# Four buffers for the projections' weights, constants issued by GpSimd, and a new order at three places of a fused block kernel

## The chip, the cores and the metric

The kernel runs on one core of one Trainium2 chip, in a single launch. The metric is the time of an execution on the device in microseconds (us); lower is better. The core has five engines that matter here: TensorE (PE in the profile, PEld for its weight loads), VectorE (DVE), ScalarE (ACT), GpSimd (POOL) and SyncE (SP, which only issues transfers). Each engine works through its own list of instructions in order and waits on semaphores. Transfers are issued from the queues of SP, ScalarE and GpSimd.

## The reference

Two transformer blocks, one after the other, on 1024 tokens of width 1024, all in float32; the second has 256 context tokens in front (1280 rows in all, in 10 tiles of 128). The change touches these pieces:

```python
# three projections, each with a residual and a norm (proj1, proj2, proj3)
x = layer_norm_affine(ALPHA * x + gate1 * (y @ w_o[l]), ln1_g[l], ln1_b[l])
y_l = concatenate([ret_o, rw_o], axis=-1) @ w_out          # even layer
# preparation of the recurrence
def token_shift_mix(u, mu):
    prev = jnp.pad(u[:, :-1], ((0, 0), (1, 0), (0, 0)))
    nxt = jnp.pad(u[:, 1:], ((0, 0), (0, 1), (0, 0)))
    return u + mu * (0.5 * (prev + nxt) - u)
w_log = -jax.nn.softplus(-(w0[d] + jnp.tanh(wd[:, :, d]) @ w2[d])) - 0.5   # low rank 64
a = jax.nn.sigmoid(a0[d] + ad[:, :, d] @ a2[d])                            # low rank 64
# recurrence in two directions, then a norm per head, a bonus and a gate
gn = ((rw_y - mean) * lax.rsqrt(var + RWKV_GN_EPS)).reshape(bl, l, RWKV_W) * rw_ln_w + rw_ln_b
rw_o = (gn + bonus.reshape(bl, l, RWKV_W)) * jax.nn.silu(u[..., E_WZ:E_SHIFT])
```

## The kernel before

`program` runs some twenty stages one after the other, with a barrier of all engines between two. In a stage each engine runs the same hand-written order of steps (`in_order`), takes the steps that concern it, and waits on counting semaphores. The change touches three stage functions.

**project_stage** is called three times (proj1 with `w_o`, proj2 with `even_w_out`, proj3 with `odd_w_out`). It multiplies 8 or 10 tiles of 128 rows by a 1024 x 1024 weight, in split precision: a weight chunk of 128 x 1024 (8 chunks, 512 KB each) is loaded into `raw` (2 buffers, loads at L639), copied to `w_hi` by ScalarE (L723) and subtracted into `w_lo` by VectorE (L772); chunk k may be loaded when `w_lo` of chunk k-2 is done. Each tile of x is transposed on TensorE ("turn", L679), split into `y_hi` (ScalarE, L731) and `y_lo` (VectorE, L811), and multiplied ("mult", three products per chunk, L690 to L692) in two halves of 512 columns; for tile 0, half 0, TensorE waits for `w_lo` chunk by chunk. ScalarE copies the product to `r` (L745), GpSimd multiplies it by the gate (L651), VectorE adds the residual `res` (loads at L628) and norms it ("norm", L822 on), and TensorE transposes it back ("back", L699). The order is turn 0, turn 1, mult 0, turn 2, norm 0, mult 1, back 0, and so on. With `gates` (proj3 alone) ScalarE first takes the silu of a second input z (L719), for tiles 0 and 1 before everything else, for tile t+2 within mult t, and VectorE multiplies it onto x (L768). The constants (gate rows, each sent to all 128 partitions, and columns of scale, shift and weight as 1024 single elements each) are issued from ScalarE's queue ahead of its other work (L706 to L714); VectorE's `fold` (L778) uses them after the last `w_lo`. proj1 has five of them, proj2 eight, proj3 two.

**rwkv_prep_stage** mixes each of 10 tiles with its neighbour rows (loads of `near` at L2245 and L2248; "shift" L2434 to L2441, "mix" L2444), makes four low-rank products ("lora", L2365; of the sequence 0,0 0,1 1,0 in step lora and 1,1 in step lora_end, through a ring of three banks), takes their sigmoid ("lora_out"), and fills the waits with other work in `slot`s: a small network with two sines ("sine", L2330 and L2427), eight scalings of filter products by a decay table ("filter" L2338 on TensorE, "scale" L2505 on VectorE, tables loaded at L2259 into two buffers), and 16 spectra ("spec", 16 matmuls each, L2350; "spec_out" L2521). Two boundaries of the sequence fall into tiles 1 and 2: there one neighbour row comes from elsewhere, and the other 127 rows are one load.

```python
for t in range(NTA):
    more = t + 1 < NTA
    yield "slot", SLOTS * t
    ...
    yield "lora_end", t
    yield "lora_out", t
    if more:
        yield "shift", t + 1
    yield "slot", SLOTS * t + 1
```

**rwkv_stage** runs 20 units (10 tiles, two directions) through a software pipeline, `PERIOD`: pairs of a step and how many units ahead it runs. T1_out (L3064) and X2 (L2857) lie on the chain of a unit, as does the trip of the inverse through memory (inv_out L2722, inv_in L2731, then X0, L2840). Behind it the two directions of a tile are added, normed per head, and gated in the y_ steps, for tile number k in the order `DONE`, in the iteration `GATED[k]`: y_load, y_load_z (SP, L2740, L2747), y_center (L3071 to L3077), y_square, y_var, y_root (ScalarE, with the silu of z before it), y_scale, y_end (L3090 to L3096, stored by GpSimd, L2784).

## Time and profile before

| | |
|---|---|
| median of 3 runs | 5418.17 us (5416.61 to 5421.66) |
| the profiled execution's own time | 5423.96 us |
| its span | 5422.3 us |
| mean granted TensorE clock | 0.891 of full speed |
| TensorE (PE) busy | 4482.0 us (83%), 26314 instructions |
| VectorE (DVE) busy | 2563.2 us (47%) |
| ScalarE (ACT) busy | 1400.6 us (26%) |
| GpSimd (POOL) busy | 643.7 us (12%) |
| proj1, proj2, proj3: first load issued at | 1048.67, 4012.53, 5277.12 us |
| preparation, recurrence: first load issued at | 2901.94, 3276.61 us |

The profile is of one execution. Times in it are microseconds from its start. A line such as L690 is a line of the kernel, printed above. "idle before <- releaser" names what ended the idle time of an engine; SPq and ACTq are the queues from which SP and ScalarE issue transfers, and the time of such a row is that of the issue alone.

### The profile page before, as it was taken

How to read it: one execution, taken by the hardware profiler on the slowest of the kernel's cores; microseconds unless marked ns; L12 is line 12 of the kernel's file. 1: busy time of each engine (PE TensorE's matmuls, PEld its weight loads, DVE VectorE, ACT ScalarE, POOL GpSimd, SP SyncE). 2: the span in 40 equal slices, each digit the busy share in tenths (PEclk: the TensorE clock that was granted, in tenths of full speed). 3: DMA queues.
4: the chain of work that ended last, by engine and by line, in shares of the span. 5: the costliest groups of instructions: out<-in, count | busy, mean ns of one | idle time of the engine just before them, and what ended most of it. 6: DMA issues, size and time to landing. Idle time of an engine off the chain costs nothing. (4 is left out here: it accounts for less than half of the span.)

```text
span 5422.3 us, 70452 instructions
## 1 busy us (share of the span) xinstructions
PE 4482.0 (83%) x26314; PEld 3681.0 (68%) x26314; DVE 2563.2 (47%) x4721; ACT 1400.6 (26%) x2867; POOL 643.7 (12%) x704
## 2 busy tenths in 40 slices
PE   5999998677998992499955686999848999886877
PEld 3998886566887882499943234888846999334546
DVE  3567774653433004311145675777534255343655
ACT  3232234432221001211122232344324111002333
POOL 1111111210000001000012012111111134110001
PEclk8999997788999996699976688999769999888998
DMA  4444433412112012222122554343332344333014
GB/s 151 164 146 146 133 110 140 169 66 58 48 46 65 30 37 105 88 79 78 56 94 105 190 216 126 99 113 105 82 107 102 124 165 173 138 129 103 8 29 142
DMA packets 430205, 578.47 MB, mean 107 GB/s; under 512 B 186461, under 2 KB 325590, under 8 KB 425256
## 3 DMA queue, kind: packets, MB, share of 16 engines
q1 hardware_dynamic: 367037, 403.73, 23.6%
q0 software_dynamic: 45280, 163.46, 7.9%
q10 hardware_dynamic: 17616, 7.66, 0.6%
q8 instruction: 171, 2.80, 0.2%
q14 instruction: 101, 0.82, 0.0%
HBM read 412.89 MB, written 161.86 MB: 106 GB/s over the span
## 5 line engine op out<-in xcount | busy, mean ns | idle before, releaser
L336 PE MATMUL g_in_g_acc<-g_in_g_whi,g_in_hi 128*128 128x444 f32 (+4 forms) x960 | 355.8, 371 | 16.4 <-DVE g_in_g_wlo L326 9.9
L337 PE MATMUL g_in_g_acc<-g_in_g_wlo,g_in_hi 128*128 128x444 f32 (+4 forms) x960 | 345.1, 359 | 0.0
L338 PE MATMUL g_in_g_acc<-g_in_g_whi,g_in_lo 128*128 128x444 f32 (+4 forms) x960 | 344.7, 359 | 0.0
L212 PE MATMUL g_even_acc<-g_even_w_hi,h_hi 128*128 128x384 f32 (+1 forms) x960 | 317.2, 330 | 30.2 <-DVE g_even_w_lo L254 30.2
L212 PE MATMUL g_down_acc<-g_down_w_buf,fT 128*128 128x256 f32 x1408 | 306.2, 381 | 16.4 <-DMA g_down_w_buf<-in_w_down 16.4
L214 PE MATMUL g_even_acc<-g_even_w_lo,h_hi 128*128 128x384 f32 (+1 forms) x960 | 317.1, 330 | 0.0
L215 PE MATMUL g_even_acc<-g_even_w_hi,h_lo 128*128 128x384 f32 (+1 forms) x960 | 317.1, 330 | 0.0
L212 PEld LDWEIGHTS g_down_acc<-g_down_w_buf,fT 128*128 128x128 f32 x1408 | 268.9, 191 | 53.7 <-DMA g_down_w_buf<-in_w_down 16.8
L336 PE MATMUL g_odd_g_acc<-g_odd_g_whi,h_hi 128*128 128x344 f32 (+3 forms) x816 | 264.9, 325 | 32.2 <-DVE g_odd_g_o L356 16.5
L337 PE MATMUL g_odd_g_acc<-g_odd_g_wlo,h_hi 128*128 128x344 f32 (+3 forms) x816 | 263.0, 322 | 0.0
L338 PE MATMUL g_odd_g_acc<-g_odd_g_whi,h_lo 128*128 128x344 f32 (+3 forms) x816 | 262.2, 321 | 0.0
L1784 DVE SCALAR_TENSOR_TENSOR up_cv<-up_acc,up_taps,up_cv 128x1023 f32<-128x1023 f32 x88 | 112.8, 1282 | 280.6 <-ACT up_cv L1760 273.3
L1739 PE MATMUL up_acc<-h_hi,up_w_hi 128*128 128x512 f32 x704 | 219.1, 393 | 8.7 <-DVE up_w_lo L1777 8.7
L230 DVE COPY g_even_o_buf<-g_even_acc 128x384 f32<-128x384 f32 (+1 forms) x60 | 32.1, 535 | 399.2 <-PE g_even_acc L215 399.2
L336 PEld LDWEIGHTS g_in_g_acc<-g_in_g_whi,g_in_hi 128*128 128x128 f32 x960 | 182.4, 190 | 56.0 <-issue 27.7
L1739 PE MATMUL up_acc<-h_lo,up_w_hi 128*128 128x512 f32 x704 | 220.2, 394 | 0.0
L1739 PE MATMUL up_acc<-h_hi,up_w_lo 128*128 128x512 f32 x704 | 218.0, 391 | 0.0
L1588 DVE SCALAR_TENSOR_TENSOR g_in_m_acc<-g_in_m_w,g_in_c_act,g_in_m_acc 128x256 f32<-128x256 f32 x448 | 201.8, 481 | 22.3 <-issue 1.9
L690 PE MATMUL proj_acc<-proj_w_hi,proj_y_hi 128*128 128x512 f32 x416 | 176.2, 424 | 32.7 <-DVE proj_w_lo L772 32.7
L212 PEld LDWEIGHTS g_even_acc<-g_even_w_hi,h_hi 128*128 128x128 f32 x960 | 181.5, 189 | 30.6 <-DVE g_even_w_lo L254 30.6
L338 PEld LDWEIGHTS g_in_g_acc<-g_in_g_whi,g_in_lo 128*128 128x128 f32 x960 | 182.4, 190 | 7.5
L337 PEld LDWEIGHTS g_in_g_acc<-g_in_g_wlo,g_in_hi 128*128 128x128 f32 x960 | 182.6, 190 | 6.5
(542 smaller groups left out, 9914.7 us busy)
## 6 DMA issues: line engine op xcount, KB each, us to landing
g_in_m_w<-in_ada_w SPq DMA_DIRECT2D x24, 1024.0 KB, 5.3
up_w_buf<-in_w_up SPq DMA_DIRECT2D x44, 512.0 KB
U2p<-g_even_o_buf POOLq DMA_DIRECT2D x11, 1920.0 KB, 7.8
g_odd_x<-U3p SPq DMA_DIRECT2D x24, 768.0 KB
g_even_w_buf<-in_even_w_in SPq DMA_DIRECT2D x11, 1536.0 KB
g_in_m_w<-in_w_ada SPq DMA_DIRECT2D x16, 1024.0 KB, 6.2
prep_near<-U2p SPq DMA_DIRECT2D x18, 896.0 KB
PD<-prep_od POOLq DMA_DIRECT2D x10, 1536.0 KB, 8.7
```

The costliest lines, as they stand in the source:

```text
L212: mm = pe.matmul(o, hi[:, k, tt], w_hi[:, par, k, :wd], start=k == 0, stop=not split and k == kc - 1)
L214: pe.matmul(o, hi[:, k, tt], w_lo[:, par, k, :wd], start=False, stop=False)
L215: mm = pe.matmul(o, lo[:, k, tt], w_hi[:, par, k, :wd], start=False, stop=k == kc - 1)
L230: op = eng.tensor_copy(o_buf[:, par, t, :wd], acc[bank][:, :wd])
L336: pe.matmul(bank[:, :wd], hi[:, k, tt], w_hi[:, st % 2, k, :wd], start=k == 0, stop=False)
L337: pe.matmul(bank[:, :wd], hi[:, k, tt], w_lo[:, st % 2, k, :wd], start=False, stop=False)
L338: op = pe.matmul(bank[:, :wd], lo[:, k, tt], w_hi[:, st % 2, k, :wd], start=False, stop=k == KC - 1)
L690: pe.matmul(acc[t % 2][hf][:], y_hi[:, t % 2, k, :], w_hi[:, k, cs], start=k == 0, stop=False)
L1588: dve.scalar_tensor_tensor(acc, w, c_act[:, k, c:c + 1], acc, ALU.mult, ALU.add)
L1739: op = pe.matmul(acc[par][side][:, cols], wt[:, par, side, k, :], ht[:, k, cols], start=k == 0 and wt is w_hi and ht is hi, stop=k == KC - ...
L1784: dve.scalar_tensor_tensor(cv[:, side, lag:], acc[par][side][:, :SEQ - lag], taps[:, tap, col], cv[:, side, lag:], ALU.mult, ALU.add)
```

## The change

In project_stage the weights go through four buffers: `raw` has two, and the residual's two buffers hold chunks 2, 3, 6 and 7. Chunk k waits for `w_lo` of chunk k-4; x of tile 1 is loaded after chunk 3 (it was after chunk 1), and the residual's first two loads wait for the last `w_lo` (they stood among the weights). The constants are issued by GpSimd, in the same order.

In rwkv_prep_stage the second sine comes before the first low-rank products. All four products of a tile are made in step lora, into four banks; the transposed low part `pt` has no bank of its own, but shares the fourth, so its transposes wait until VectorE has emptied the banks. The first two decay tables are loaded ahead of the second tile's rows, and the 127 rows at a boundary are loaded as 112 and 15.

In rwkv_stage the last two tiles leave the pipeline: their y_ steps run after it, in pairs (`ALONE`). The last of them has buffers of its own, borrowed from inputs that are no longer in use (`xr`, `xk`, `ew`), and semaphores of its own. From iteration 18 on the order is `ENDING`: y_end, y_load_z, y_center, y_square and y_bonus come behind T1_out. The silu of z is a step of its own, at the same place.

```diff
@@ project_stage @@
+        w_in = (s.w0, s.w1, s.w2, s.w3)
+        raw_of = lambda k: (raw if k % 4 < 2 else res)[:, k % 2]
...
             for k in range(KC):
-                if k >= 2:
-                    sp.wait_ge(s.w_lo, k - 1)
-                sp.dma_start(raw[:, k % 2], w_v[:, k, :]).then_inc((s.w_even, s.w_odd)[k % 2], DMA)
-                if k == 1:
+                if k >= 4:
+                    sp.wait_ge(s.w_lo, k - 3)
+                sp.dma_start(raw_of(k), w_v[:, k, :]).then_inc(w_in[k % 4], DMA)
+                if k == 3:
                     load_x(1)
-                if k in (3, 5):
-                    load_res(k // 4)
+            sp.wait_ge(s.w_lo, KC)
+            load_res(0)
+            load_res(1)
             in_order(step)
...
+            for m, k in enumerate(kinds):
+                pool.dma_start(gate_rows[:, m], k.gate.partition_broadcast(P)).then_inc(s.const, DMA)
...
         def _(act):
-            for m, k in enumerate(kinds):
-                act.dma_start(gate_rows[:, m], k.gate.partition_broadcast(P)).then_inc(s.const, DMA)
...
@@ rwkv_prep_stage @@
         yield "norm", 0
+        yield "sine", 1
         yield "lora", 0
-        yield "sine", 1
...
-            yield "lora_end", t
...
-        pt = ps("pt", [P, 2, P])
-        ring = [ps(f"ring{n}") for n in range(3)]
+        ring = [ps(f"ring{n}") for n in range(4)]
+        pt = ring[3][:, 0:2 * P].rearrange("p (n t) -> p n t", n=2)
...
+                    row, most, rest = (0, (16, P), (1, 16)) if n == 0 else (P - 1, (0, P - 16), (P - 16, P - 1))
+                    sp.dma_start(near[row:row + 1, par, n], U2p[0:1, U_SHIFT:EVEN_IN]).then_inc(done, DMA)
+                    for a, b in (most, rest):
+                        sp.dma_start(near[a:b, par, n], U2p[first + a:first + b, U_SHIFT:EVEN_IN]).then_inc(done, DMA)
...
                     sp.dma_start(mu_r[:], mu.partition_broadcast(P)).then_inc(s.mu, DMA)
+                    load_dec(0)
+                    load_dec(1)
                     load_near(1)
                     load_x(1)
-                    load_dec(0)
-                    load_dec(1)
...
                 if what == "low":
                     pe.wait_ge(s.tanh, t + 1)
+                    if t:
+                        pe.wait_ge(s.freed, 4 * t)
...
-                    for n, d in ((0, 0), (0, 1), (1, 0)) if what == "lora" else ((1, 1),):
...
-                        if use >= 3:
-                            pe.wait_ge(s.freed, use - 2)
-                        pe.matmul(ring[use % 3][:], tT[half, n, :], lw[half, n, :], start=True, stop=True).then_inc(s.ring, 1)
+                    for n, d in ((0, 0), (0, 1), (1, 0), (1, 1)):
+                        half = slice(d * 64, (d + 1) * 64)
+                        pe.matmul(ring[2 * n + d][:], tT[half, n, :], lw[half, n, :], start=True, stop=True).then_inc(s.ring, 1)
...
@@ rwkv_stage @@
-    for u in DONE[2:]:
+    for u in DONE[2:NTA - 2]:
         GATED.append(max(GATED[-1] + 1, 2 * passed[u] + 3))
...
+    LATER = ("y_end", "y_load_z", "y_center", "y_square", "y_bonus")
+    sums_at = PERIOD.index(("T1_out", 0))
+    ENDING = tuple(p for p in PERIOD[:sums_at] if p[0] not in LATER) + PERIOD[sums_at:sums_at + 1]
+    ENDING += tuple(p for p in PERIOD if p[0] in LATER) + PERIOD[sums_at + 1:]
+    ALONE = (("y_load", 0), ("y_load_z", 0), ("y_center", 0), ("y_square", 0), ("y_bonus", 0), ("y_silu", 0), ("y_var", 0), ("y_root", 0), ("y_scale", 0), ("y_end", 0))
...
-            for what, ahead in PERIOD:
+            for what, ahead in ENDING if at >= UNITS - 2 else PERIOD:
...
+        for what, ahead in ALONE:
+            for k in (NTA - 2, NTA - 1):
+                part(what, k, DONE[k], k % 2)
...
-                    wait(sp, s.y_var, n)
+                    if n == NTA - 1:
+                        sp.wait_ge(s.ew, UNITS)
+                    else:
+                        wait(sp, s.y_var, n)
```

## Rows read from the trace of the kernel before

**Rows 1.** Waits of the first projection: us, times, longest

```profile
ACT proj_w_hi L723 <- DMA proj_raw<-in_w_o: 14.7, 6, 4.9
```

**Rows 2.** Timeline of the first projection: start, duration, operation, count, [idle before]

```profile
1058.57 1.97 PE L679 MATMUL proj_pt<-ident,proj_x 128*128 128x128 f32 x8 [2.67 <-DMA proj_x<-Y]
...
1059.99 1.46 SPq L639 DMA_DIRECT2D proj_raw<-in_w_o  x2
...
1080.67 1.23 DVE L772 TENSOR_TENSOR proj_w_lo<-proj_raw,proj_w_hi 128x1024 fp32r<-128x1024 f32 x1 [1.78 <-ACT proj_w_hi L723]
...
1083.40 0.63 PE L690 MATMUL proj_acc<-proj_w_hi,proj_y_hi 128*128 128x512 f32 x1
...
1084.68 0.63 PE L690 MATMUL proj_acc<-proj_w_hi,proj_y_hi 128*128 128x512 f32 x1
...
1090.43 1.03 PE L679 MATMUL proj_pt<-ident,proj_x 128*128 128x128 f32 x8
```

**Rows 3.** The same view of the second projection's start

```profile
4017.77 1.97 PE L679 MATMUL proj_pt<-ident,proj_x 128*128 128x128 f32 x8 [43.46 <-DMA proj_x<-YB]
...
4025.08 1.08 ACT L731 ACTIVATE proj_y_hi<-proj_pt 128x512 fp32r<-128x512 f32 x2 [19.93 <-issue]
...
4057.68 1.03 PE L679 MATMUL proj_pt<-ident,proj_x 128*128 128x128 f32 x8
```

**Rows 4.** The same view of the third projection's start

```profile
5291.61 1.06 ACT L719 ACTIVATE proj_z<-proj_z 128x1024 f32<-128x1024 f32 x1 [4.18 <-DMA proj_z<-U3p]
...
5320.02 1.06 ACT L719 ACTIVATE proj_z<-proj_z 128x1024 f32<-128x1024 f32 x1 [2.71 <-DMA proj_z<-U3p]
...
5326.28 1.03 PE L679 MATMUL proj_pt<-ident,proj_x 128*128 128x128 f32 x8
```

**Rows 5.** Timeline of VectorE in the preparation

```profile
2948.50 1.33 DVE L2427 TENSOR_SCALAR prep_ws<-prep_acc,prep_cols 64x1024 f32<-64x1024 f32 x1 [15.73 <-PE prep_acc L2330]
...
3008.87 2.48 DVE L2505 TENSOR_TENSOR prep_z<-prep_acc,prep_ws 128x512 f32<-128x512 f32 x4 [20.24 <-DMA prep_ws<-in_t_decay]
```

**Rows 6.** Waits of VectorE in the preparation, from 3009 us on

```profile
DVE prep_sg L2471 <- PE prep_ring L2365: 24.0, 8, 4.2
```

**Rows 7.** Timeline of TensorE at the preparation's start

```profile
2934.97 0.69 PE L2355 MATMUL prep_pt<-ident,prep_td 128*128 128x128 f32 x2 [26.56 <-ACTq L2392]
2941.00 3.77 PE L2365 MATMUL prep_ring<-prep_lw,prep_tT 64*128 64x512 f32 x6 [5.35 <-DMA prep_kar<-in_rw_ka]
2944.71 3.67 PE L2330 MATMUL prep_acc<-prep_ws,prep_w2s 64*64 64x512 f32 x4
```

**Rows 8.** Timeline of SP's queue in the preparation

```profile
2952.93 26.63 SPq L2248 DMA_DIRECT2D prep_near<-U2p  x2
```

**Rows 9.** Timeline of TensorE in the preparation's later tiles

```profile
3143.98 7.13 PE L2350 MATMUL prep_acc<-prep_z,prep_ws 128*128 128x512 f32 x16
...
3160.09 9.79 PE L2350 MATMUL prep_acc<-prep_z,prep_ws 128*128 128x512 f32 x16
...
3170.87 7.13 PE L2350 MATMUL prep_acc<-prep_z,prep_ws 128*128 128x512 f32 x16
```

**Rows 10.** Timeline of TensorE in the recurrence's last units

```profile
3913.34 1.97 PE L2857 MATMUL rwkv_wx<-rwkv_T,rwkv_A 64*64 64x64 f32 x16 [5.11 <-DVEq L3066]
...
3923.28 1.98 PE L2840 MATMUL rwkv_wx<-rwkv_T,rwkv_A 64*64 64x64 f32 x32 [0.77 <-ACT rwkv_TF L2964]
```

**Rows 11.** Windows of the first projection: us, busy of each engine, PEclk, DMA share, GB/s

```profile
1052.00:1055.00 3.00, 1.06 (x5) 1.06 (x6) 0.00 (x0) 0.00 (x0) 0.00 (x0) 0.50 1.00 362
```

**Rows 12.** The strided load that GpSimd issues, by its source line

```profile
L1356 POOL DMA_DIRECT2D g_in_pos_i<-in_positions x1: 916/916/916, 57.8 to 57.8; - x1
```

**Rows 13.** Loads of 128 rows in the preparation, from issue to landing

```profile
DMA to landing us min/median/max: 5.4/6.0/58.0
```

**Rows 14.** Timeline of SP's queue in the recurrence's last units

```profile
3915.45 1.27 SPq L2731 DMA_DIRECT2D rwkv_T<-TD  x2
```

**Rows 15.** Timeline of GpSimd at the recurrence's end

```profile
3988.12 0.57 POOL L2784 DMA_DIRECT2D YB<-rwkv_yx  x1 [3.15 <-DVE rwkv_yx L3096]
```

More of the change, by code:

```diff
@@ L565, in project_stage @@
     n_cols = sum((k.scale is not None) + (k.shift is not None) + (k.weight is not None) for k in kinds)
-    with stage(nc, name, "const", "cols", "w_even", "w_odd", "w_hi", "w_lo", "x_even", "x_odd", "silu", "gated", "turned", "y_hi", "y_lo", "mm", "r_out", "r_free",
+    with stage(nc, name, "const", "cols", "w0", "w1", "w2", "w3", "w_hi", "w_lo", "x_even", "x_odd", "silu", "gated", "turned", "y_hi", "y_lo", "mm", "r_out", "r_free",
                "r_gated", "res_even", "res_odd", "var", "std", "normed", "xn", "back", "h", "h_hi", "h_lo", "kept_even", "kept_odd") as (block, s, sb, ps):
@@ L660, in step @@
                         pool.dma_start(tiles[t].keep, xn[:]).then_inc(kept(t), DMA)
+            for m, k in enumerate(kinds):
+                pool.dma_start(gate_rows[:, m], k.gate.partition_broadcast(P)).then_inc(s.const, DMA)
+                for c, v in enumerate((k.scale, k.shift, k.weight)):
+                    if v is not None:
+                        pool.dma_start(cols[:, m, c, :], col_view(v), allow_slow_non_contiguous=True).then_inc(s.const, DMA)
+            if affine:
+                pool.dma_start(g_row[:], affine[0].partition_broadcast(P)).then_inc(s.const, DMA)
+                pool.dma_start(b_row[:], affine[1].partition_broadcast(P)).then_inc(s.const, DMA)
+            if final is not None:
+                pool.dma_start(f_row[:], final.partition_broadcast(P)).then_inc(s.const, DMA)
             pool.wait_ge(s.const, DMA * (n_rows + n_cols))
@@ L771, in weights @@
                 dve.wait_ge(s.w_hi, k + 1)
-                dve.tensor_tensor(w_lo[:, k], raw[:, k % 2], w_hi[:, k], ALU.subtract).then_inc(s.w_lo, 1)
+                dve.tensor_tensor(w_lo[:, k], raw_of(k), w_hi[:, k], ALU.subtract).then_inc(s.w_lo, 1)
             def fold():
@@ L2240, in load_near @@
                     sp.wait_ge(s.mixed, t - 1)
+                done = (s.near_even, s.near_odd)[par]
                 for n in range(2):
-                    first, end, cut = t * P + 2 * n, (t + 1) * P + 2 * n, t == NTC - n
-                    row = 0 if n == 0 else P - 1
-                    if cut:
-                        sp.dma_start(near[row:row + 1, par, n], U2p[0:1, U_SHIFT:EVEN_IN]).then_inc((s.near_even, s.near_odd)[par], DMA)
-                        first, end = (first + 1, end) if n == 0 else (first, end - 1)
-                    a = 1 if cut and n == 0 else 0
-                    sp.dma_start(near[a:a + end - first, par, n], U2p[first:end, U_SHIFT:EVEN_IN]).then_inc((s.near_even, s.near_odd)[par], DMA)
+                    first = t * P + 2 * n
+                    if t != NTC - n:
+                        sp.dma_start(near[:, par, n], U2p[first:first + P, U_SHIFT:EVEN_IN]).then_inc(done, DMA)
+                        continue
+                    row, most, rest = (0, (16, P), (1, 16)) if n == 0 else (P - 1, (0, P - 16), (P - 16, P - 1))
+                    sp.dma_start(near[row:row + 1, par, n], U2p[0:1, U_SHIFT:EVEN_IN]).then_inc(done, DMA)
+                    for a, b in (most, rest):
+                        sp.dma_start(near[a:b, par, n], U2p[first + a:first + b, U_SHIFT:EVEN_IN]).then_inc(done, DMA)
             def store_rv(t):
@@ L2356, in part @@
                     op.then_inc(s.turned, 1)
-                if what in ("lora", "lora_end"):
+                if what == "lora":
                     if t == 0:
```

93 lines of the change are left out of this document (51 added, 42 removed), and 2 rows, old and new, of the table PERIOD.

## The prediction, made before the changed kernel was run

> **What bounds the kernel.** I read the page first. In the table above TensorE is busy 83% of the span, so only a place where TensorE waits, or a stage that another engine paces, can give time. The change touches three functions. For them I read the waits, then the timeline, asking in each place whose idle time ends last and what ended it.
>
> *Projections (three calls).* In the first call ScalarE waits 14.7 us in 6 waits for weight chunks [rows 1]; the other two look alike. With two buffers the third chunk is asked for only when the first one's low part is done: ask, land, copy, subtract, about 6 us for each pair. The third and fourth are asked for at 1059.99 and the last low part begins at 1080.67, while TensorE needs 1.28 us for a chunk at the lower clock (1083.40 to 1084.68). It is through tile 0 at 1090.43, where it turns tile 2 [rows 2]. So tile 0 is bound by the latency of eight loads, two at a time. In the second call TensorE turns tile 0 at 4017.77, but ScalarE copies it only from 4025.08, because eight constants are issued from its queue first; tile 2 is turned at 4057.68 [rows 3]. In the third tile 2 is turned at 5326.28 [rows 4].
>
> *Preparation.* VectorE sets its pace. It waits 15.73 us for the second sine's product and 20.24 us for a decay table [rows 5] (a shorter wait for the first table lies between), and 24.0 us in 8 waits for the fourth low-rank product [rows 6]. The sine's product stands on TensorE behind tile 0's low-rank products, which wait for a constant until 2941.00 [rows 7]. The decay table stands in SP's queue behind the 127-row load of the neighbours, whose issue takes 26.63 us [rows 8]. The fourth product stands behind 16 matmuls of a spectrum, up to 9.79 us [rows 9].
>
> *Recurrence, last units.* TensorE waits 5.11 us, in two units, for VectorE's T1_out, which stands behind y_end and y_center [rows 10].
>
> **The change part by part.** Times are those of the profiled execution: 5423.96 us, span 5422.3, 5.8 us above the median 5418.17.
>
> *Projection 1.* Four chunks go out at once, then x of tile 1. Ahead of that x's landing stand 3.1 MB (x0, four chunks, x1) instead of 2.1, and the constants' 1.6 MB. At the 362 GB/s of [rows 11] 3.1 MB take 8.7 us and 4.7 MB 13 us; counted from 1051, two us behind the first issue, x1 lands between 1059.7 and 1064. It landed at 1058.57 [rows 2]. TensorE turns tile 1 before it multiplies, so its start slips: that is the price. I take 1063.5, and the multiplication from 1065.5. Meanwhile chunks 4 to 7 are asked for about 1.3 us apart (VectorE's pace, 1.23 us each [rows 2]) from 1059 on and land behind x1; the last low part ends near 1072. Half 0 then ends at 1073 to 1076. Half 1 took 7.0 us, 1083.40 to 1090.43, the clock rising within it; it takes 5.4 if it has risen before, 10.2 if not. End 1078.5 to 1084, most likely 1080.5: gain 10, bounds 6 and 12. A rule speaks against this part: the Trainium skill (DMA: Bandwidth & Descriptors, Queues, rings and completion order) says each DMA engine takes turns between the queues it has work for. By it the constants, now in GpSimd's queue from the start, share with the weights: x1 lands at the late end and the gain is 9; weights served first would make it 12.
>
> The residual's loads go behind the last low part. Residual 0 lands near 1076, used after half 1: nobody waits. x of tile 2 queues behind both and lands near 1078.5: 0 to 1 us, inside the bounds.
>
> *Projection 2.* The same, and ScalarE no longer issues eight constants, so it copies tile 0 from about 4019. x1 lands near 4026, the multiplication starts at 4027.7, the last low part ends at 4034, half 1 at 4040 to 4046 against 4057.68. Gain 15, bounds 11 and 18.
>
> *Projection 3.* On ScalarE the silu of x1 stands before the first copy. It started at 5291.61 [rows 4] and now waits for 1 MB more, 2.8 us, so the last low part ends at about 5309.5. Behind it go two residuals and then x and z of tile 2, whose silu started at 5320.02 and would start at 5317.4; tile 2 is turned at 5319.8, after a wait of 2 to 4 us (that is what is late next). 5326.28 - 5319.8 = 6.5, less 1.5 for a lower clock after the pause: 5, bounds 1 and 9.
>
> *Constants from GpSimd.* A strided load of 1024 single elements takes 0.916 us of GpSimd's queue [rows 12], so eight constants take under 7.4 us there. GpSimd has no other work before tile 0's product, and the consumer, fold, comes after all low parts. Price 0, bounds 0 and 4; if the cover goes, VectorE's y_lo of tile 1 is late by the excess.
>
> *Preparation, sine 1 before lora 0.* TensorE is done turning at 2935.7 (2934.97 + 0.69); the two sine products take 3.67 us [rows 7], to 2939.4. VectorE, which began at 2948.50, begins at 2939.5. Gain 9.0, the filter's products follow. The wait for the first table is worth 0: the same group ends with TensorE's fourth filter product in either order.
>
> *Decay tables first, and the 127 rows cut into 112 and 15.* Nothing slow stands before the table, so the 20.24 us go. What is late next is TensorE, whose filter products start at about 2974: 2.0 us come back. Gain 18.2. No row shows a load of 112 or 15 rows. The nearest are the full 128 rows, 6.0 us to landing (median) [rows 13], and the 127 rows, over 26 us of queue; with the second price the gain is 0. I take the first, as 112 of 128 rows lie nearest to it. The Trainium skill (same page, Why a DMA increments its semaphore by 16 and not by 1) gives a rule: the number of engines is the largest up to 16 that divides the rows. By it 127 rows go through 1, 112 through 16, 15 through 15.
>
> *Four low-rank products together.* The 8 waits of 24.0 us go; the longest, 4.2 us, belongs to the last tile, where TensorE's own chain ends the stage, and is worth nothing. 19.8, and 1 for tile 0's, before that window. VectorE's period, 26.9 us (3143.98 to 3170.87), falls to about 22.7. TensorE's (turn 0.7, wait 0.5, four products 5.0, spectra 9.2 and 7.13 [rows 9]) is 22.5: they meet, so the lower bound is 12. The turn's new wait, for the shared bank, is over before it: VectorE empties the bank a whole shift and mix earlier. Preparation: 9.0 + 18.2 + 20.8 = 48, bounds 35 and 52.
>
> *Recurrence.* With T1_out first, X2 starts 3.6 us earlier, twice. In the first unit it is lost: y_end ends 2.4 us later, SP's loads of z wait for it, and the loads of the inverse, behind them in SP's queue, went out from 3915.45 [rows 14] and landed near 3921.4; X0 started at 3923.28 and would start at 3923.8: 0.5 lost. In the second no X0 follows: 3.6 gained. The last two tiles run as a pair, but tile 9's load waits for the store issued at 3988.12 [rows 15] to land, and tile 8's z stands behind it on SP; stepped through, the pair ends 0.5 later. 3.6 - 0.5 - 0.5 is about 3, bounds -2 and 8.
>
> Sum: 10 + 15 + 5 + 48 + 3 = 81. 5424 - 81 = 5343 profiled, **5337** for the median.
>
> **Rivals.**
> 1. *TensorE paces the preparation.* VectorE's ring waits become waits for spectra, and of 20.8 us 3 are left. For it: both periods come to 22.5. Against: TensorE idles some 4 us per tile, and with less idling two spectra take 14.3 instead of 16.9. Time 5337 + 18 = 5355. 13%.
> 2. *The cut does not spread.* The table still stands behind a slow load: 18.2 less, 5355. 4%.
> 3. *The projections become bound by transfers.* 5 MB and constants in 20 us come near [rows 11]; if x1 is served last and the chunks behind it, they give 10 instead of 30: 5357. 12%.
> 4. *Slower: the clock.* If TensorE stays at 1.2 GHz through the spectra, each takes 14.3 us, not 7.13 [rows 9]: a period of 34.8 against 26.9, over 7 tiles 55 us, and 14 on the last two: 69. Against that 29 gained before, 18 in projections at that clock, 3: 5418 + 19 = 5437. It decides once about three quarters of the 16 are slow. Against it: in each tile the second spectrum already runs at the higher clock, and idling falls. 3%.
>
> **How the numbers follow.** Forecast 65%, 5337, own range 5317 to 5356. Rivals 1 to 3 29%, at 5355 to 5375 and their pairs up to 5390; rival 4 3%; unforeseen 3%. The range 5310 to 5373 leaves out some 6% below and 12% above. A measurement of this kernel can tell 0.2%, 11 us, from no change: faster 0.94, same 0.02, slower 0.04.
>
> **What would show it.** Right: under 5 us of waits for weight chunks in a call; tile 2 turned 10, 15 and 5 us sooner after each call's first issue; no decay wait over 3 us, no ring wait, a period near 22.7 us; X0 of unit 19 no earlier. Wrong: x of tile 1 over 6 us later, a new wait of VectorE for spectra, the 112-row load taking over 10 us, fold waiting for constants.

## Result, and the profile after

The changed kernel takes **5333.55 us** (median of 4 runs, 5328.30 to 5336.91) against 5417.39 (4 runs, 5414.93 to 5421.66) for the kernel before on the same chip: ratio 0.984, 95% interval 0.9824 to 0.9857. 83.8 us faster, and 3.5 us below the forecast of 5337. The profiled executions took 5423.96 us before and 5332.88 after: 91.1 us apart, where the sum was 81.

The page, its span and TensorE's row (busy us, share, instructions):

```profile
span 5331.0 us, 70443 instructions
...
PE 4419.6 (83%) x26314; PEld 3649.4 (68%) x26314; DVE 2562.9 (48%) x4721; ACT 1397.0 (26%) x2865; POOL 654.7 (12%) x719
```

To see where the time went, I take each stage from its first load to the next stage's first load:

| stretch | before | after | difference | predicted |
|---|---|---|---|---|
| first projection, and what follows up to the preparation | 1853.3 | 1843.2 | -10.1 | -10 |
| preparation | 374.7 | 319.7 | **-55.0** | -48 |
| recurrence | 735.9 | 724.2 | **-11.7** | -3 |
| second projection, and what follows | 1264.6 | 1249.5 | -15.1 | -15 |
| third projection | 145.2 | 142.4 | -2.8 | -5 |

What is left up to the difference of the spans (91.3) is +3.4 in the stages ahead of the first projection, which the change doesn't touch. The same kernel's stages vary by a few us from one execution to the next, as the experiments show; that is the size of doubt of each row.

Timeline of the first projection after the change (start, duration, queue or engine, line):

```profile
1060.70 2.90 SPq L641 DMA_DIRECT2D proj_raw<-in_w_o  x2
...
1067.29 1.97 PE L692 MATMUL proj_pt<-ident,proj_x 128*128 128x128 f32 x8 [9.46 <-DMA proj_x<-Y]
...
1074.95 1.22 DVE L774 TENSOR_TENSOR proj_w_lo<-proj_res,proj_w_hi 128x1024 fp32r<-128x1024 f32 x1 [1.43 <-ACT proj_w_hi L725]
...
1082.49 1.03 PE L692 MATMUL proj_pt<-ident,proj_x 128*128 128x128 f32 x8
```

These answer to [rows 2]. Counted from the stage's first load (1052.02, before 1048.67), x of tile 1 is turned at 15.3 us instead of 9.9, the last low part begins at 22.9 instead of 32.0, and tile 2 is turned at **30.5 instead of 41.8**. The price and the gain can both be read here: TensorE waits 9.46 us for x of tile 1, 6.8 more than before, and is still done with tile 0 11.3 us sooner. ScalarE's waits for weight chunks fell from 14.7, 14.4 and 14.5 us in the three calls to 8.1, 9.3 and 5.2: not under 5 in any of them, which the prediction had named as a sign of being right.

The same of the second projection (first load at 3939.09), with two of GpSimd's issues of constants:

```profile
3940.05 1.79 POOL L668 DMA_DIRECT2D proj_cols<-mod  x2
3941.83 0.88 POOL L668 DMA_DIRECT2D proj_cols<-in_norm_w  x1
...
3956.27 1.97 PE L692 MATMUL proj_pt<-ident,proj_x 128*128 128x128 f32 x8 [11.61 <-DMA proj_x<-YB]
...
3970.47 1.03 PE L692 MATMUL proj_pt<-ident,proj_x 128*128 128x128 f32 x8
```

Tile 2 is turned 31.4 us after the first load, before 45.2 [rows 3]: 13.8 sooner. Third projection (first load at 5188.58):

```profile
5205.60 1.06 ACT L721 ACTIVATE proj_z<-proj_z 128x1024 f32<-128x1024 f32 x1 [6.51 <-DMA proj_z<-U3p]
...
5230.90 1.06 ACT L721 ACTIVATE proj_z<-proj_z 128x1024 f32<-128x1024 f32 x1 [9.06 <-DMA proj_z<-U3p]
...
5233.27 1.09 PE L692 MATMUL proj_pt<-ident,proj_x 128*128 128x128 f32 x8 [3.73 <-DVE proj_x L770]
```

The second silu begins at 17.0 instead of 14.5, and tile 2 is turned at 44.7 instead of 49.2, behind a new wait of 3.73 us [rows 4].

VectorE's waits in the preparation (engine, tile, line, what ended them: us in total, times, longest):

```profile
DVE prep_z L2508 <- PE prep_acc L2341: 16.2, 16, 2.3
...
DVE prep_ws L2430 <- PE prep_acc L2333: 6.6, 1, 6.6
DVE prep_ws L2524 <- ACT prep_odd L2418: 5.9, 2, 3.6
DVE prep_near L2440 <- DMA prep_x<-U2p: 3.4, 2, 2.6
```

No wait for a decay table and none for the ring is left; the sine's has gone from 15.73 to 6.6 us [rows 5, 6]. (A ring wait is one for a low-rank product in the ring of banks.) The loads that held SP's queue for 26.63 us [rows 8] now read

```profile
2898.69 1.00 SPq L2262 DMA_DIRECT2D prep_ws<-in_t_decay  x2
...
2917.89 0.29 SPq L2249 DMA_DIRECT2D prep_near<-U2p  x1
2918.22 0.81 SPq L2251 DMA_DIRECT2D prep_near<-U2p  x2
```

(L2251 issues the 112 and the 15 rows). And TensorE in the later tiles:

```profile
3131.18 0.44 PE L2360 MATMUL prep_ring<-ident,prep_td 128*128 128x128 f32 x2 [3.08 <-ACTq L2395]
...
3135.56 14.00 PE L2353 MATMUL prep_acc<-prep_z,prep_ws 128*128 128x512 f32 x32
3153.74 0.69 PE L2360 MATMUL prep_ring<-ident,prep_td 128*128 128x128 f32 x2 [4.19 <-ACTq L2395]
...
3181.24 21.71 PE L2353 MATMUL prep_acc<-prep_z,prep_ws 128*128 128x512 f32 x48
```

The period is 22.56 us (3131.18 to 3153.74; predicted 22.7, before 26.9), two spectra take 14.0 instead of 16.9 [rows 9], and TensorE still idles 3 to 4 us in each, while VectorE is busy for 21.2 of the 22.56 us (3131.18 to 3153.74): VectorE paces the stage, not TensorE.

The recurrence's last units, answering to [rows 10, 14]:

```profile
3844.33 0.32 SPq L2770 DMA_DIRECT2D rwkv_yv<-PC  x1
...
3845.69 0.59 SPq L2737 DMA_DIRECT2D TD<-rwkv_inv  x1
...
3856.26 1.97 PE L2866 MATMUL rwkv_wx<-rwkv_T,rwkv_A 64*64 64x64 f32 x32 [6.72 <-DMA rwkv_TT<-TD]
...
3876.66 1.14 PE L2883 MATMUL rwkv_wx<-rwkv_T,rwkv_A 64*64 64x64 f32 x16 [1.42 <-DVEq L3096]
```

The wait for T1_out is 1.42 us instead of 5.11, and X2 behind it takes **1.14 us instead of 1.97**. (Before, three units wait 5.11 us, not two: 17, 18 and 19. The change leaves unit 17 as it was.) X0 of unit 19 waits 6.72 us for the inverse, whose store SP issues behind the loads of z: what the first of the two units gained is lost there.

### The profile page after: what moved, and what is told of

It is laid out like the page before. It is cut to its first block and busy times, and to the rows that moved or that the text cites. A ratio compares the mean times of both kernels' runs of the same rounds, so it can differ in the third digit from the quotient of the medians.

```text
span 5331.0 us, 70443 instructions
## 1 busy us (share of the span) xinstructions
PE 4419.6 (83%) x26314; PEld 3649.4 (68%) x26314; DVE 2562.9 (48%) x4721; ACT 1397.0 (26%) x2865; POOL 654.7 (12%) x719
## 5 line engine op out<-in xcount | busy, mean ns | idle before, releaser
L212 PEld LDWEIGHTS g_down_acc<-g_down_w_buf,fT 128*128 128x128 f32 x1408 | 269.0, 191 | 53.9 <-DMA g_down_w_buf<-in_w_down 16.9
L336 PE MATMUL g_odd_g_acc<-g_odd_g_whi,h_hi 128*128 128x344 f32 (+3 forms) x816 | 263.6, 323 | 34.1 <-DVE g_odd_g_o L356 18.2
L230 DVE COPY g_even_o_buf<-g_even_acc 128x384 f32<-128x384 f32 (+1 forms) x60 | 32.1, 535 | 399.1 <-PE g_even_acc L215 399.1
L212 PEld LDWEIGHTS g_even_acc<-g_even_w_hi,h_hi 128*128 128x128 f32 x960 | 181.5, 189 | 30.5 <-DVE g_even_w_lo L254 30.5
L336 PEld LDWEIGHTS g_odd_g_acc<-g_odd_g_whi,h_hi 128*128 128x128 f32 x816 | 156.6, 192 | 42.3 <-DVE g_odd_g_o L356 19.8
```

Source lines behind the costliest of these rows:

```text
L212: mm = pe.matmul(o, hi[:, k, tt], w_hi[:, par, k, :wd], start=k == 0, stop=not split and k == kc - 1)
L230: op = eng.tensor_copy(o_buf[:, par, t, :wd], acc[bank][:, :wd])
L336: pe.matmul(bank[:, :wd], hi[:, k, tt], w_hi[:, st % 2, k, :wd], start=k == 0, stop=False)
```

## The experiments

Each experiment changes the kernel before (the first four) or the changed kernel. The runs lie on three chips, on which the kernel before took 5422.20 us (the first four), 5420.82 (x early, rows late, 64 and 63, z behind the inverse) and 5418.64 (the others); the ratios compare on one chip, the forecasts of the first four took it as 5417 to 5418. Beside times, three readings are compared: the length of a stage as above; the intervals between GpSimd's 20 stores of O in the recurrence, one per unit; and, in a projection, when tile 2 is turned, counted from the stage's first load.

### One part at a time

**The recurrence alone.**

```diff
-            for what, ahead in PERIOD:
+            for what, ahead in ENDING if at >= UNITS - 2 else PERIOD:
...
+        for what, ahead in ALONE:
+            for k in (NTA - 2, NTA - 1):
+                part(what, k, DONE[k], k % 2)
```

> The kernel before with the recurrence's part of the change alone. The stage (its first load to the second projection's first load) took 735.9 us before and 724.2 us after. Theory A: of these 11.7 only 5 to 7 belong to the edit: in the last unit X2 no longer waits 5.11 us, and because TensorE waits 1.4 us instead its clock stays at 2.4 GHz, so the matmuls behind it keep their short times too (5 us in the unit), and 1 us comes from the pair at the end; the other 4 to 6 come from where the clock happens to rise at the stage's head. Stage 729 to 731, X2 of the last unit 1.14 us, X0 of the last unit no earlier against the unit before; whole time 5411 to 5413. Theory B: everything belongs to the edit: stage 724, whole time 5406. Theory C, the prediction's sum: 3 us, stage 733, X2 of the last unit still 1.97 us; whole time 5415.

Measured: 5415.57 us, ratio 0.999 (0.998 to 0.9999); stage 724.3. The last two stores of O:

```profile
3933.72 0.57 POOL L2792 DMA_DIRECT2D RW<-rwkv_O  x1 [18.76 <-ACT rwkv_O L2998]
3961.93 0.57 POOL L2792 DMA_DIRECT2D RW<-rwkv_O  x1 [13.48 <-ACT rwkv_O L2998]
```

The last interval is 28.2 us. Which theory holds is seen only beside the other runs. In the four profiles in which the recurrence is unchanged (before, and the next three experiments) the stage takes 735.9, 730.7, 728.3 and 732.7 us, and the last interval 33.2 in all four. So the last unit gained **5.1 us**, repeatably: 28.0 to 28.2 in the seven profiles whose last unit has this order and z where the change has it. The rest of the 11.7 lies mostly at the stage's start, which nobody touched: over all runs the first store of O comes 98.9 to 103.5 us after it, and the same 16 transposes there take from 1.97 to 3.68 us. The interval before the last tells nothing: 32.3 to 33.7 with the order, 32.1 to 33.6 without. The tail behind the last store is 39.1 to 41.0 us in those seven with the pair, 39.5 to 40.8 in the four without: nothing that can be read either. Theory A's mechanism holds, and so does its gain of 5 to 7 in the whole time (6.6 us by the medians on this chip, in an interval that all but reaches no change); its stage length (729 to 731) does not, within that spread.

**The cut alone.**

```diff
...
+                    row, most, rest = (0, (16, P), (1, 16)) if n == 0 else (P - 1, (0, P - 16), (P - 16, P - 1))
...
+                    for a, b in (most, rest):
+                        sp.dma_start(near[a:b, par, n], U2p[first + a:first + b, U_SHIFT:EVEN_IN]).then_inc(done, DMA)
```

> The kernel before with the 127 rows loaded as 112 and 15, and nothing else; the decay tables stay behind the second tile's rows. The preparation took 374.7 us before. Theory A: the cut alone takes the 20.24 us wait and most of the 4.84 us wait away, because nothing slow is left in SP's queue: preparation 351 to 356, each of the 112-row and 15-row issues under 2 us. Theory B: the order of the tables earns it, the cut alone only shortens the issue: preparation 365 to 372. Whole time 5395 to 5399 by A, 5409 to 5416 by B.

**The decay tables alone.**

```diff
                     sp.dma_start(mu_r[:], mu.partition_broadcast(P)).then_inc(s.mu, DMA)
+                    load_dec(0)
+                    load_dec(1)
                     load_near(1)
                     load_x(1)
-                    load_dec(0)
-                    load_dec(1)
```

> The kernel before with the first two decay tables loaded ahead of the second tile's rows, and nothing else; the 127 rows stay one load. Theory A: only the wait for the first table goes (4.84 us; some of it comes back as waits for the filter's products), the 20.24 us wait stays, since its table is issued behind the second load of 127 rows whatever the order at the start: preparation 370 to 374 instead of 374.7. Theory B: the order earns most of the 22 us: preparation 352 to 358. Whole time 5414 to 5418 by A, 5396 to 5401 by B.

**Four products and four banks alone.**

```diff
...
-                    for n, d in ((0, 0), (0, 1), (1, 0)) if what == "lora" else ((1, 1),):
...
+                    for n, d in ((0, 0), (0, 1), (1, 0), (1, 1)):
...
```

> The kernel before with all four low-rank products of a tile in step lora and four banks, and nothing else. VectorE waited 25.1 us for the fourth products in all. Theory A: all of it is gained, the last tile's too, because the last spectra start when VectorE has made their inputs: preparation 349 to 351, whole time 5393 to 5395. Theory B, the prediction's step: 20.8, the last tile's 4.2 being worth nothing: preparation 354, whole time 5397. Theory C, TensorE paces the stage once the waits go: 3 gained, preparation 371, new waits of VectorE for spectra.

| | preparation | ratio to before |
|---|---|---|
| before | 374.7 | |
| cut | 349.7 | 0.9954 (0.9938 to 0.9971) |
| tables first | 374.8 | 1.0002 (0.9991 to 1.0014) |
| four products | 347.6 | 0.9956 (0.9939 to 0.9972) |
| all, with the sine's order | 319.7 | |

The cut earns 25.0 us by itself and the order of the tables nothing: theory A's mechanism in both, though both stages lie about 1 us outside its ranges (351 to 356, 370 to 374). With the tables first, SP's queue is held even longer (30.16 us for 26.63), and VectorE waits 23.9 us once for the table behind it, where it waited 4.8 and 20.2. SP's queue, then VectorE's waits, of that kernel:

```profile
2947.47 30.16 SPq L2248 DMA_DIRECT2D prep_near<-U2p  x2
```

```profile
DVE prep_z L2505 <- DMA prep_ws<-in_t_decay: 23.9, 1, 23.9
```

The four products earn 27.1, somewhat more than theory A's 25. Both alone also go with a shorter wait for the second sine. That wait in the kernel with the cut, then in the one with the four products:

```profile
DVE prep_ws L2429 <- PE prep_acc L2332: 10.9, 1, 10.9
```

```profile
DVE prep_ws L2426 <- PE prep_acc L2329: 13.8, 1, 13.8
```

15.7 before. But a shorter wait there is not yet a gain: with the tables first it fell to 11.3 us too, and the stage stayed at 374.8. What a part is worth is read at VectorE's first product with `kar` (L2480 in the kernel before, in tile 0's lora_out), which stands behind the sine and the first tables. Counted from the stage's first load it begins at

| | first product with `kar` | from there to the stage's end |
|---|---|---|
| before | 116.9 | 257.7 |
| cut | 94.8 | 254.8 |
| four products | 116.7 | 230.9 |
| all, with the sine's order | 89.0 | 230.7 |

So the cut acts ahead of this point (22.1 us) and the four products behind it (26.9). All together gain 27.9 ahead of it, 5.8 more than the cut alone: that is the most that the sine's order, which wasn't run alone, can have earned. Behind it they gain 27.1, hardly more than the four products alone, though the cut by itself gained 2.9 there: this much doesn't add up.

### The projections' start

**x of tile 1 early again.**

```diff
-                if k == 3:
+                if k == 1:
                     load_x(1)
```

> The changed kernel with x of tile 1 loaded after the second chunk, as before the change, in all three projections. In the first projection of the changed kernel x of tile 1 was turned 15.3 us after the first issue, the last low part began at 22.9 and tile 2 was turned at 30.5. Theory A, the start is bound by the bytes it moves (6.6 MB in some 19 us), so their order does not matter: tile 1 is turned at about 10 to 12, but the last low part begins at 22.5 to 23.5 and tile 2 is turned at 30 to 31.5; whole time as the changed kernel's, 5331 to 5336. Theory B, the late x of tile 1 is what costs (TensorE waits 9.5 and 11.6 us for it): tile 2 is turned 3 to 5 us sooner in the first two projections, whole time 5323 to 5328.

Measured: 5330.98 us, ratio 0.9837 (0.9822 to 0.9853), as the changed kernel. Tile 1 is turned at 11.2 and 12.3 us, the last low part begins at 24.0 and 24.7, and tile 2 is turned at 32.3 and 32.2: 1.8 and 0.8 us **later** than with the late x. Theory B falls for these two, and A is near (it had tile 2 at 30 to 31.5). In the third projection, where ScalarE's silu of tile 1 stands ahead of the copies, it is the other way round: tile 2 at 41.4 instead of 44.7, stage 139.2 instead of 142.4.

**The broadcast rows late.**

```diff
...
+            pool.wait_ge(s.w_lo, 5)
             for m, k in enumerate(kinds):
                 pool.dma_start(gate_rows[:, m], k.gate.partition_broadcast(P)).then_inc(s.const, DMA)
...
```

> The changed kernel with the broadcast rows among the constants (gate, gain, bias: 0.5 MB each, three, four and two of them) issued by GpSimd only when five low parts are done; the small columns still go out at the start, and the fold waits for them alone. Theory A, the start is bound by bytes: 1.5, 2 and 1 MB at the 345 GB/s seen there no longer stand beside the weights, so tile 2 is turned 4, 5 and 2 us sooner than in the changed kernel (30.5, 31.4 and 44.7 us after the first issue), and nobody waits for the rows, since the first product of the gate comes 9 us after their issue: whole time 5320 to 5325. Theory B, the next bound is the chain of copy, subtraction and TensorE at the low clock: 1 to 2 us each, whole time 5328 to 5331. Theory C, the rows come late and GpSimd's first product waits: no gain or a loss of some us.

Measured: 5322.74 us, ratio 0.9824 (0.981 to 0.9837). In the first projection GpSimd's issue, and TensorE's turn of tile 2:

```profile
1068.18 0.56 POOL L670 DMA_DIRECT2D proj_gate_rows<-mod  x1 [12.99 <-DVE proj_w_lo L776]
...
1080.96 1.09 PE L694 MATMUL proj_pt<-ident,proj_x 128*128 128x128 f32 x8 [1.32 <-DMA proj_x<-Y]
```

The last low part begins at 19.0 us, 3.9 sooner, as bytes have it (1.5 MB at 345 GB/s are 4.3). But tile 2 is turned only 2.5 us sooner (28.0), and 1.9 in each of the other two. In the first two calls TensorE now waits for x of tile 2 (1.32 and 0.44 us), which is issued after the late rows; that it is held up by them is argued from the order, not tried apart. By the turns this lies between A and B. The time lies in A's range, but its interval overlaps the changed kernel's (0.9824 to 0.9857), so the time alone doesn't decide. A window of the changed kernel's first projection, and the same of this one (us, busy of each engine, granted clock, DMA share, GB/s), show both near the 362 GB/s of [rows 11]:

```profile
1054.00:1073.50 19.50, 8.18 (x34) 6.92 (x34) 9.94 (x9) 8.49 (x9) 1.86 (x3) 0.59 0.92 341
```

```profile
1055.00:1071.00 16.00, 8.66 (x30) 7.22 (x31) 9.87 (x9) 8.63 (x10) 1.80 (x4) 0.53 0.96 347
```

**The constants from ScalarE again.**

```diff
         def _(act):
+            for m, k in enumerate(kinds):
+                act.dma_start(gate_rows[:, m], k.gate.partition_broadcast(P)).then_inc(s.const, DMA)
...
```

> The changed kernel with the projections' constants issued by ScalarE again; the four buffers stay. In the second projection ScalarE then issues eight constants (some 7 us) before it copies tile 0 and the first chunk; in the changed kernel the first low part begins 7.2 us after the first issue, the last at 23.8, tile 2 is turned at 31.4. Theory A, the start is bound by bytes, which the queue does not change: the first low part begins at 10 to 15, but four chunks have landed by then and are worked off at VectorE's pace (1.3 us instead of 2.5), so the last begins at 23.5 to 26 and tile 2 is turned at 31 to 34; first and third projection within 1.5 us; whole time 0 to 5 above the changed kernel's 5333. Theory B, the copies are what bounds: all of the second projection moves by the 5 to 7 us that the first copy is late, tile 2 at 37 to 39; whole time 5339 to 5343.

Measured: 5341.27 us, ratio 0.9852 (0.9837 to 0.9867). In the second projection:

```profile
3939.23 7.52 ACTq L712 DMA_DIRECT2D proj_cols<-in_norm_w  x1
...
3953.04 1.08 ACT L734 ACTIVATE proj_y_hi<-proj_pt 128x512 fp32r<-128x512 f32 x2 [25.83 <-issue]
```

One issue takes 7.52 us, and ScalarE copies tile 0 only 15.3 us after the first load. Tile 2 is turned at 38.4 instead of 31.4: theory B, 7.0 us. First and third projection: 31.0 and 45.6, within a us.

### The load of 127 rows

The changed kernel, with the 127 rows loaded as 64 and 63 instead of 112 and 15.

```diff
-row, most, rest = (0, (16, P), (1, 16)) if n == 0 else (P - 1, (0, P - 16), (P - 16, P - 1))
+row, most, rest = (0, (64, P), (1, 64)) if n == 0 else (P - 1, (0, 64), (64, P - 1))
```

> The changed kernel with the 127 rows loaded as 64 and 63 instead of 112 and 15. Theory A, as the Trainium skill has it (DMA: Bandwidth & Descriptors): the largest number up to 16 that divides the rows is 9 for 63, so the load still spreads: preparation 319 to 322 us, as with 112 and 15 (319.7), each issue under 2 us. Theory B: only a multiple of 16 rows spreads, 63 go through one engine like the 127: their load holds SP's queue for 8 to 13 us each time, and the preparation takes 322 to 332 us.

```profile
2913.19 0.29 SPq L2249 DMA_DIRECT2D prep_near<-U2p  x1
2913.52 1.03 SPq L2251 DMA_DIRECT2D prep_near<-U2p  x2
```

Both loads of a pair are issued within 1.03 us, the preparation takes 319.5 us (319.7 with 112 and 15), the whole 5333.07 (ratio 0.9848, 0.9832 to 0.9864). Theory A. 63 rows are no multiple of 16 and do not hold the queue, 127 do. That is what the Trainium skill's rule (DMA: Bandwidth & Descriptors, Why a DMA increments its semaphore by 16 and not by 1) says of 63 and 127; which engines moved them was not read.

### The inverse and the loads of z

**The late order from unit 17 on, z where it was.**

```diff
-            for what, ahead in ENDING if at >= UNITS - 2 else PERIOD:
+            for what, ahead in ENDING if at >= UNITS - 3 else PERIOD:
```

> The changed kernel with its late order from unit 17 on instead of 18, and the loads of z where the change has them, ahead of the inverse in SP's queue. With the z loads behind the inverse as well, the last three intervals between the stores of O went from 35.6, 33.7, 28.1 to 30.4, 28.4, 28.0 us. Theory A: the position of the z loads is what earns this, and T1_out first is given back in every unit that is followed by an X0, since y_end and with it the z loads and the inverse come later: intervals 34 to 37, 33 to 34.5, 28; stage within 2 us of the changed kernel's 724 to 727. Theory B: T1_out first earns its 3.6 us and the clock in unit 17 whatever SP does: first interval 30 to 31.5, stage 719 to 721.

Measured: 5336.12 us, ratio 0.9853 (0.9838 to 0.9869), stage 725.6, last intervals 37.2, 32.9, 28.2. Unit 17's wait for T1_out is 1.42 us, and then

```profile
3809.95 0.67 SPq L2737 DMA_DIRECT2D TD<-rwkv_inv  x1
...
3819.39 1.97 PE L2866 MATMUL rwkv_wx<-rwkv_T,rwkv_A 64*64 64x64 f32 x32 [8.12 <-DMA rwkv_TT<-TD]
```

TensorE waits 8.12 us for the inverse. Theory A, each interval within 0.2 us of its range: the gain is given back in the next unit's X0.

**The same, with z behind the inverse.**

```diff
+    FROM = UNITS - 3
-    LATER = ("y_end", "y_load_z", "y_center", "y_square", "y_bonus")
+    LATER = ("y_end", "y_center", "y_square")
...
+    ENDING = kept_order(PERIOD[:read_at]) + (("y_load_z", 1), ("y_bonus", 1)) + kept_order(PERIOD[read_at:sums_at + 1])
+    ENDING += tuple(p for p in PERIOD if p[0] in LATER) + kept_order(PERIOD[sums_at + 1:])
...
```

> The changed kernel with the recurrence's late order from unit 17 on instead of 18, and in it the loads of z (and GpSimd's bonus) behind the loads of the inverse instead of ahead of them in SP's queue. In the changed kernel TensorE waits 5.11 us for T1_out in unit 17, works at 1.2 GHz behind that, and waits 6.72 us for the inverse in unit 19; the last three intervals between the stores of O are 35.6, 33.7 and 28.1 us. Theory A: the inverse is ready 8 us before its store is issued, and only y_end and the loads of z, which wait for it, stand ahead in SP's queue. Both waits go, and with them the low clock: X0 of unit 18 starts 5 to 8 us sooner against unit 17's store, X0 of unit 19 4 to 5 us sooner; stage 710 to 715 instead of 724.2, whole time 5319 to 5325. Theory B: the trip through memory is itself the bound, and what the queue gives back is lost there: stage 719 to 724, whole time 5328 to 5334. Theory C: z lands too late, ScalarE stands in its silu and TensorE waits for U: stage 724 or more.

```profile
3798.98 0.59 SPq L2741 DMA_DIRECT2D TD<-rwkv_inv  x1
...
3802.66 1.14 PE L2887 MATMUL rwkv_wx<-rwkv_T,rwkv_A 64*64 64x64 f32 x16 [1.42 <-DVEq L3100]
...
3805.25 0.62 SPq L2774 DMA_DIRECT2D rwkv_yv<-PC  x1
...
3811.12 1.97 PE L2870 MATMUL rwkv_wx<-rwkv_T,rwkv_A 64*64 64x64 f32 x32 [1.42 <-ACT rwkv_TF L2994]
```

The inverse's store is now issued 3.7 us ahead of X2, where it was 5.7 behind it in the run above, and X0 no longer waits for it: what ended its 1.42 us is ScalarE's copy. Last intervals **30.4, 28.4, 28.0** instead of 35.6, 33.7, 28.1, stage 712.3 instead of 724.2; 5324.78 us, ratio 0.9829 (0.9816 to 0.9842). In six profiles with z ahead of the inverse and the late order from unit 18 on, these three intervals add up to 95.5 to 97.5 us, here to 86.9 and in the next experiment to 86.6: a gain of about 9 to 11 us. Theory A, but for one step: the low clock did not go with the two waits. This X0 takes 1.97 us like the one that had waited 8.12, at a granted clock of 0.50; X1 of unit 17, 32 products of the same shape at a granted clock of 1.00, took 1.15.

### Together

Rows late, z behind the inverse from unit 17 on, and x and z of tile 1 early in the third projection alone (`if k == (1 if gates else 3)`):

> The changed kernel with three edits together: the broadcast rows issued after five low parts, the late order from unit 17 on with the loads of z behind the inverse, and x and z of tile 1 loaded after the second chunk in the third projection alone. Alone they were worth 8 to 10, 12 and 3 us by the stages. Theory A, they lie in different stages or shorten different waits and add: tile 2 turned at 28, 29.5 and 39.5 to 41.5 us in the three projections, recurrence 710 to 716, whole time 5307 to 5313. Theory B, they overlap in the third projection, where fewer bytes leave nothing for the order: tile 2 there at 42 to 43, whole time 5312 to 5316.

Measured: **5317.02 us** (5309.35 to 5320.35), ratio **0.9807 (0.9794 to 0.9821)**. Tile 2 is turned at 28.4, 29.1 and 40.6 us, the last intervals are 30.4, 28.2, 28.0, the recurrence takes 716.5, the third projection 139.4. So the parts add where they act, as theory A has it, and tile 2 of the third projection (40.6) speaks against B. The whole time lies 4 us above A's range, though, and just above B's too. Against the changed kernel's 0.984 (0.9824 to 0.9857) the intervals do not meet: this version beats both, by about 16 us and 100 us of the medians.

The same with the late order from unit 15 on (`FROM = UNITS - 5`):

> As the three edits together, but with the late order from unit 15 on. In unit 16 TensorE waits 1.55 us for T1_out and works at a granted clock of 0.86 around it, in unit 15 it does not wait for it. Theory A: the 1.55 us go and the clock stays up: the interval before the store of unit 16 (35.6 us before) is 2 to 4 shorter, stage 708 to 712. Theory B: in a full unit TensorE has other work to put there, and the later y_end costs as much as it gives: stage 711 to 715, time as the other version within 3 us. Theory C: with y_center behind T1_out in units that still make pairs, VectorE is late for the pairs: new waits, stage 714 to 720.

Measured: 5327.11 us, ratio 0.9828 (0.9815 to 0.9842), stage 723.9; the intervals before the stores of units 15 and 16 grow from 33.5 and 35.6 to 37.0 and 40.2. The waits between 3700 and 3830 us, and those of all engines between 3725 and 3790:

```profile
PE rwkv_f L2861 <- ACT rwkv_arT L2965: 11.6, 2, 6.3
...
POOL rwkv_yv L2809 <- DMA rwkv_yz<-U2p: 17.2, 2, 12.9
```

Slower by 10 us than the version before it. In a full unit the z loads, behind the inverse, land late (GpSimd waits 12.9 us), and TensorE waits 11.6 us for ScalarE's copies arT, on whose queue the silu of z stands. The loss is of theory C's kind and larger (723.9 lies above its 714 to 720), and the late engine is ScalarE, not VectorE. That the silu is what holds ScalarE is argued from the order, not tried apart.

## Why the prediction was right

The mechanism was right in the main: each wait that was to go did go or shrink, and most of what was named as late next was. That the total came within 3 us is partly luck. The readings below add up to 89.7 us (11.3 + 13.8 + 4.5 + 55.0 + 5.1), 9 more than the sum of 81, and the two profiled executions differ by 91.1. But the profiled execution before lay 6.6 us above its median, and the one after 0.7 below; the prediction had taken 5.8 off both alike. These 7 us bring the difference of the medians back to 83.8.

Part by part, the medians on one chip give 6.6 us for the recurrence alone, 26.3 for the cut and 25.3 for the four products. The projections' start was never run alone, so its 30 us rest on the readings within the stages.

- *Projection 1, gain 10 (6 to 12).* 11.3 by the turn of tile 2, 10.1 by the stretch. x of tile 1 was taken to land so that its turn comes 14.8 us after the first load; it came at 15.3. The cost on that side was real and the gain larger, as argued.
- *Projection 2, gain 15 (11 to 18).* 13.8. The multiplication began 18.8 us after the first load instead of the 15.2 taken, since x of tile 1 came later with eight constants beside it. The two causes were rightly kept apart: of the 13.8, 7.0 are the constants' move.
- *Projection 3, gain 5 (1 to 9).* Tile 2 4.5 sooner, after a wait of 3.73 us where 2 to 4 were forecast; the stage itself 2.8 shorter. The late x and z were taken to cost 2.8 us here and cost 3.3; loaded early they need not have.
- *The queues.* The rule of the Trainium skill that each DMA engine takes turns between its queues (DMA: Bandwidth & Descriptors, Queues, rings and completion order) had x of tile 1 at the late end and the gain at 9. x did come at the late end, and with the rows away it is turned at 11.4 instead of 15.3; the gain was not 9 but 10 to 11.
- *Weight chunks.* "Under 5 us of waits for weight chunks in a call" failed: 8.1, 9.3 and 5.2. The chunks were to come at VectorE's pace of 1.3 us; in the first call the low parts begin about 2.5 us apart up to the fifth. With the broadcast rows away the waits are 4.4, 6.6 and 4.7: here transfers set the pace more than the sum allowed. The gain did not suffer by it.
- *Constants from GpSimd, price 0.* 0.88 us for a strided load (taken: 0.916), none waited for.
- *Preparation, 48 (35 to 52).* 55.0: the direction right, the size missed by 7, and outside the bounds. Ahead of VectorE's first product with `kar` the sum held: 9.0 + 18.2 = 27.2, measured 27.9, though shared out otherwise (22.1 for the cut, at most 5.8 for the sine), since the queue that the cut frees also carries the first table, and "the wait for the first table is worth 0" was wrong: 4.84 us became 2.26. The mis-sized term is the four products, 20.8 against 27.1. "The longest, 4.2 us, belongs to the last tile, where TensorE's own chain ends the stage, and is worth nothing": from that first product with `kar` to the last tile's, all 24.0 us of the ring waits are gained, the 4.2 too, because that chain got shorter as well, 26.6 us from the turn to its last product (3176.31 to 3202.95) instead of 29.7 (3233.75 to 3263.42). Its three spectra take 21.71 us instead of 9.75 and 14.00, and its low-rank products 3.78 instead of 3.78 and 1.12. Beyond that VectorE waits 3.7 us less for the filter's products and 1.5 more for x in that stretch.
- *The tables' order* was counted together with the cut; it is worth nothing.
- *Recurrence, 3 (-2 to 8).* 5.1. "In the first unit it is lost: 0.5" held in direction: X0 of unit 19 starts 35.2 us behind X0 of unit 18, before 34.7. A loss as small as 0.5 can't be read, since this distance is 33.7 to 35.2 in the profiles with the order and 33.4 to 34.7 in those without. "In the second 3.6 gained" was short: the step counted the wait and not what TensorE's clock does behind it. The pair at the end, taken as -0.5, is worth nothing that can be read.

The rivals: TensorE does not pace the preparation (it idles 3 to 4 us a tile, VectorE 1.4); the cut spreads; in the projections the bytes do set the pace now (341 GB/s), but with the gain in hand; the mean granted clock rose from 0.891 to 0.902 instead of falling.

## What to carry to other kernels

Where a load can't be spread it costs not its own landing alone but everything issued behind it on its queue; look there before reordering what waits. A wait that is moved off the critical path is only worth it if nothing that stands behind the moved step in *another* engine's queue is due: here the loads of z ahead of the inverse gave back all of one unit's gain, and moving them was worth more (9 to 11 us by the last three intervals) than the whole recurrence part of the change (5.1). When a stage's start is bound by bytes, load what is needed last, last.

## What the runs showed of the hardware

In the recurrence's last unit a wait of TensorE cost more than its length. Windows over the last unit before (from 1.8 us ahead of X2) and after the change (from 1.7 us ahead), with TensorE's busy time first and the granted clock as the third number from the end:

```profile
3946.00:3962.00 16.00, 12.82 (x72) 12.24 (x73) 4.24 (x7) 7.55 (x11) 2.31 (x2) 0.54 0.20 68
```

```profile
3875.00:3889.00 14.00, 9.71 (x81) 9.03 (x76) 6.75 (x13) 7.02 (x11) 2.85 (x3) 0.78 0.30 95
```

After 5.11 us idle the clock is down to 1.2 GHz when X2 starts (0.54 of full over the window), after 1.42 us it is still at 2.4 GHz: X2 1.97 against 1.14 us, and a pair of the products behind it 0.79 against 0.49. The whole unit gained 5.1 us where the wait shrank by 3.7. The high clock did not last: it was granted in full up to 3882 us and at half from 3884 on. Nor does the length of the last wait decide. With z behind the inverse, X0 of unit 18 followed a wait of 1.42 us too, and ran at 0.50; TensorE had waited 1.42 and 1.93 us already in the 10 us before.

A load of 127 rows held SP's queue for 26 to 30 us; as 112 and 15, or as 64 and 63, the same rows are issued in about 1 us. And the first strided load of `in_norm_w`, 1024 single elements, took 0.88 us to issue on GpSimd's queue and 7.52 on ScalarE's, with the same four chunks asked for beside it; with two chunks, in the kernel before, 5.14 on ScalarE's. The second one took 0.88 on GpSimd's queue and 1.98 on ScalarE's, so it is not a fixed price.
